# Second layer's input projection: units in the order queries, keys, latents, values, with norm, turn and eviction work spread between them

## What is computed

```
h = rms_norm(x, n1_g) * (1.0 + sc1) + sh1
z = h @ w_in                                   # 1024 -> 1952 columns
dq, dk, dv, qa, kva, kr = jnp.split(z, ODD_SPLITS, axis=-1)   # 512, 512, 512, 256, 128, 32
dq = rms_norm(dq.reshape(B, S, DIFF_HEADS, 2, DIFF_HD), dq_g)
dk = rms_norm(dk.reshape(B, S, DIFF_HEADS, 2, DIFF_HD), dk_g)
ckv = rms_norm(kva, kva_g)
q = rms_norm((rms_norm(qa, qa_g) @ w_qb).reshape(B, S, MLA_HEADS, MLA_QK), mq_g)
...
dq = apply_rope(dq, cos, sin)                  # latent tokens only
dk = apply_rope(dk, cos, sin)
lam = jnp.exp(jnp.sum(lq1 * lk1)) - jnp.exp(jnp.sum(lq2 * lk2)) + LAMBDA_INIT
o1 = attend(dq[:, :, :, 0:1], k_d[:, :, :, 0], v_d)
o2 = attend(dq[:, :, :, 1:2], k_d[:, :, :, 1], v_d)
```

## Time and profile before

| | us |
|---|---|
| median of 3 runs (lowest, highest) | 1410.58 (1409.72, 1410.68) |
| profiled execution | 1410.37 |
| its span in the trace | 1408.5 |
| TensorE busy | 1280.5 (91%) |
| VectorE busy | 896.6 (64%) |
| ScalarE busy | 758.0 (54%) |
| TensorE on the chain that ended last | 75% |

### The profile page before, as it was taken

How to read it: one execution, slowest core, us unless ns; L and a number is a source line. 1 busy time by engine, 2 the same in 40 slices (tenths; PEclk the granted TensorE clock), 3 DMA queues, 4 the chain that set the end, 5 groups by cost and what they waited for, 6 DMA issues and landing times.

```text
span 1408.5 us, 19755 instructions
## 1 busy us (share of the span) xinstructions
PE 1280.5 (91%) x7731; PEld 1125.5 (80%) x7731; DVE 896.6 (64%) x1149; ACT 758.0 (54%) x1098; POOL 293.4 (21%) x248
## 2 busy tenths in 40 slices
PE   5896899899999998987968898999999999999895
PEld 3794567799899987984656697889989989889793
DVE  1448756453433345665575524889789789799776
ACT  3467664542323225323355324677777877777673
POOL 0368850100110012000023021011312303213113
PEclk9997899999999998995986796999999999999998
DMA  9842993153443354421921121699899899899882
GB/s 311 238 134 88 303 331 122 59 165 98 143 147 106 98 170 136 125 70 62 333 64 61 31 83 47 224 332 336 263 347 322 277 337 327 277 340 319 285 294 79
DMA packets 178361, 277.67 MB, mean 197 GB/s; under 512 B 7121, under 2 KB 105193, under 8 KB 178265
## 3 DMA queue, kind: packets, MB, share of 16 engines
q1 hardware_dynamic: 176040, 269.87, 57.8%
q0 software_dynamic: 2224, 6.49, 1.7%
HBM read 274.02 MB, written 2.31 MB: 196 GB/s over the span
## 4 chain that ended last, share of the span: by engine, by line
PE 75%; DVE 10%; issue 8%; ACT 4%; DMA 2%; POOL 1%; SPq 1%; DVEq 0%; ACTq 0%; POOLq 0%
PE psB L1994 5%; PE psB L1996 5%; PE psB L1995 5%; PE psB L1497 4%; PE psB L1499 4%; PE psB L1498 4%; PE psA L1994 4%; PE psA L1996 4%; PE psA L1995 4%; PE psB L1583 3%; PE psB L1638 2%; PE psB L1733 2%; PE psB L1732 2%; PE psB L1734 2%; PE psA L1618 2%
## 5 line engine op out<-in xcount | busy, mean ns | idle before, releaser
L2619 DVE TENSOR_TENSOR Wl<-raw,Wh 128x1408 fp32r<-128x1408 f32 (+2 forms) x144 | 247.1, 1739 | 57.5 <-ACT Wh L1397 56.7
L2057 DVE TENSOR_TENSOR Wl<-raw,Wh 128x2048 fp32r<-128x2048 f32 (+4 forms) x64 | 133.9, 2097 | 141.6 <-ACT Wh L1039 141.2
L1397 ACT CAST Wh<-raw 128x1408 fp32r<-128x1408 f32 (+2 forms) x144 | 197.0, 1375 | 27.5 <-PE psA L1996 14.5
L1039 ACT CAST Wh<-raw 128x2048 fp32r<-128x2048 f32 (+4 forms) x64 | 109.9, 1724 | 116.4 <-PE psB L1734 64.2
L1994 PE MATMUL psA<-Wh,hTh 128*128 128x352 f32 x360 | 118.3, 329 | 0.7 <-ACT hTl L1403 0.7
L1996 PE MATMUL psA<-Wh,hTl 128*128 128x352 f32 x360 | 116.7, 324 | 0.0
L1995 PE MATMUL psA<-Wl,hTh 128*128 128x352 f32 x360 | 116.1, 323 | 0.0
L935 POOL TENSOR_TENSOR yc<-yc,work 128x414 f32<-128x414 f32 x90 | 101.1, 1145 | 52.8 <-ACT work L1138 50.2
L1497 PE MATMUL psB<-Wh,hTh 128*128 128x256 f32 (+2 forms) x356 | 104.2, 293 | 7.8 <-DVE Wl L2057 2.0
L1498 PE MATMUL psB<-Wl,hTh 128*128 128x256 f32 (+2 forms) x356 | 103.6, 291 | 0.0
L1499 PE MATMUL psB<-Wh,hTl 128*128 128x256 f32 (+2 forms) x356 | 103.6, 291 | 0.0
(11 more groups left out here) (376 smaller groups left out, 3398.7 us busy)
## 6 DMA issues: line engine op xcount, KB each, us to landing
raw<-in_l_moe_w SPq DMA_DIRECT2D x108, 704.0 KB, 5.7
raw<-in_l_ada_w SPq DMA_DIRECT2D x48, 1024.0 KB, 6.0
raw<-in_l_ffn_w SPq DMA_DIRECT2D x28, 1024.0 KB, 5.3
raw<-in_l_moe_w SPq DMA_DIRECT2D x27, 768.0 KB, 6.4
gate_b<-in_l_moe_w SPq DMA_DIRECT2D x18, 768.0 KB, 7.0
gate_b<-in_l_moe_w SPq DMA_DIRECT2D x18, 704.0 KB, 5.8
raw_tail<-in_l_moe_w SPq DMA_DIRECT2D x18, 704.0 KB, 5.6
raw<-in_l_w_in SPq DMA_DIRECT2D x11, 1024.0 KB, 5.6
```

The lines of the kernel that those rows point to most:

```text
L1039: act.copy(hi_of(u), raw_of(u)).then_inc(hi_ready, 1)
L1397: act.copy(half_of(Wh, h), raw_half(h)).then_inc(half_hi, 1)
L2057: dve.tensor_tensor(lo_of(u), raw_of(u), hi_of(u).bitcast(F32), ALU.subtract).then_inc(lo_ready, 1)
L2619: dve.tensor_tensor(half_of(Wl, h), raw_half(h), half_of(Wh, h).bitcast(F32), ALU.subtract).then_inc(half_lo, 1)
```

## The change

The eight units now come in the order queries, queries, keys, keys, latents, latents, values, values. VectorE empties the banks of units 0 and 1 only, ScalarE those of units 2 to 7 (18 banks), each time behind the items of that unit. All six items lie between units: 0 and 1 at unit 2, item 2 at unit 3, items 3 and 4 at unit 4, item 5 at unit 5. The latent norms lie at unit 6. TensorE makes the seven groups of `TURNS1` between units: two behind unit 3, one behind 4, three behind 5, one behind 6. Only the latents' three groups are left behind unit 7. `lam`'s sums move to VectorE's list at step 17 of `attend(0)`, its Exp to ScalarE's list there, two steps later. The writes of the new keys, values and latents to memory stay where they were in GpSimd's list.

```diff
-                unit(KD, 256, (0, w_in[:, :, 1536:1792]))
-                unit(KD, 256, (0, w_in[:, :, 1696:1952]))
-                for j in range(6):
-                    unit(KD, 256, (0, w_in[:, :, j * 256:(j + 1) * 256]))
+                for at in (0, 256, 512, 768, 1536, 1696, 1024, 1280):
+                    unit(KD, 256, (0, w_in[:, :, at:at + 256]))
...
-        Z_LAT, Z1, Z2 = NT + 1, NT + 1, 3 * NT + 1
+        Z_LAT, Z1, Z2 = 3 * NT + 1, NT, 3 * NT + 1
...
-        ITEM_AT = {4: 0, 5: 1, 6: 2, 7: 3}
+        ITEMS1 = {2: (0, 1), 3: (2,), 4: (3, 4), 5: (5,)}
+        LATENT_AT, ACT_UNITS = 6, 2
         TURNS1 = [(0, 0), (0, 1), (0, 2), (1, 0), (1, NT), (1, 1), (1, 2)]
+        TURNS1_AFTER = {3: (0, 1), 4: (2,), 5: (3, 4, 5), 6: (6,)}
...
+                    if a == 0 and s == LAMBDA_AT + 2:
+                        act.wait_ge(lam_in, 1)
+                        act.activation(stats[:, 90:92], stats[:, 88:90], ACT.Exp).then_inc(lam_e, 1)
...
-            table_of(ACT.Exp)
-            act.wait_ge(lam_in, 1)
-            act.activation(stats[:, 90:92], stats[:, 88:90], ACT.Exp).then_inc(lam_e, 1)
+            g0 = first["prep1"]["T"]
             for j in range(8):
                 if j < 7:
                     step(base["in", 1] + j)
-                if j in (1, 2):
-                    qk_root((QR, KVR)[j - 1], NT)
-                if j in ITEM_AT:
-                    act.wait_ge(psB_free, first["in1"]["B"] + NT * j)
-                    squares(1, ITEM_AT[j])
+                for n in TURNS1_AFTER.get(j - 1, ()):
+                    k, t = TURNS1[n]
+                    transposed_in(g0 + n, (qT1, kT1)[k][:, :, t * P:(t + 1) * P])
+                act.wait_ge(psB_free, first["in1"]["B"] + NT * j)
+                for m in ITEMS1.get(j, ()):
+                    squares(1, m)
+                for m in ITEMS1.get(j, ()):
                     qk_root(HD, 8)
-            g0 = first["prep1"]["T"]
-            act.wait_ge(psB_free, first["in1"]["B"] + 24)
-            squares(1, 4)
+                if j == LATENT_AT:
+                    qk_root(QR, NT)
+                    qk_root(KVR, NT)
+                if j >= ACT_UNITS:
+                    for t in range(NT):
+                        act.wait_ge(psB_full, first["in1"]["B"] + NT * j + t + 1)
+                        act.copy(in1_columns(j, t), in1_bank(j, t)).then_inc(psB_free, 1)
...
             for j in range(1, 8):
                 unit_b(base["in", 1] + j, first["in1"]["B"] + NT * j, (hTh, hTl))
-            pe.wait_ge(cache_in, 96)
+                for n in TURNS1_AFTER.get(j, ()):
+                    turn1(n)
...
-                dve.wait_ge(psB_free, first["in1"]["B"] + NT * j)
-                if j in (1, 2):
-                    at, n, name = ((0, QR, "l1_mla_q_a_norm_g"), (QR, KVR, "l1_mla_kv_a_norm_g"))[j - 1]
...
+                dve.wait_ge(psB_free, first["in1"]["B"] + NT * (j if j == LATENT_AT else min(j, 4)))
+                if j == LATENT_AT:
+                    for at, n, name in ((0, QR, "l1_mla_q_a_norm_g"), (QR, KVR, "l1_mla_kv_a_norm_g")):
...
-                if j in ITEM_AT:
-                    item1(ITEM_AT[j])
-                for t in range(NT):
...
+                for m in ITEMS1.get(j, ()):
+                    item1(m)
+                for t in range(NT) if j < ACT_UNITS else ():
+                    dve.wait_ge(psB_full, first["in1"]["B"] + NT * j + t + 1)
+                    dve.tensor_copy(in1_columns(j, t), in1_bank(j, t)).then_inc(psB_free, 1)
```

More of the change, by code:

```diff
@@ L59 @@
 OUT_SPLIT = 23
+LAMBDA_AT = 17
 AHEAD = S - 1
@@ L724, in lat_columns, with in1_columns, in1_bank @@
             return kv[:, t, j * 512:(j + 1) * 512]
-        ITEM_AT = {4: 0, 5: 1, 6: 2, 7: 3}
+        ITEMS1 = {2: (0, 1), 3: (2,), 4: (3, 4), 5: (5,)}
+        LATENT_AT, ACT_UNITS = 6, 2
         TURNS1 = [(0, 0), (0, 1), (0, 2), (1, 0), (1, NT), (1, 1), (1, 2)]
+        TURNS1_AFTER = {3: (0, 1), 4: (2,), 5: (3, 4, 5), 6: (6,)}
+        def in1_columns(j, t):
+            if j in (4, 5):
+                return zm[:, t, 0:256] if j == 4 else zm[:, t, 256:416]
+            at = j * 256 if j < 4 else (j - 2) * 256
+            return zd[:, t, at:at + 256]
+        def in1_bank(j, t):
+            n = units[base["in", 1] + j][2]
+            return psB[(first["in1"]["B"] + NT * j + t) % 3][:, n - 160 if j == 5 else 0:n]
         blocks = ([(0, d // 2 + YC * (d % 2)) for d in range(FRONT)] + [(0, u) for u in range(FRONT, ADA)] +
@@ L1855, in _, with turn1 @@
             norm(1, 0, rows_products(base["in", 1], first["in1"]["B"]))
+            def turn1(n):
+                k, t = TURNS1[n]
+                g = first["prep1"]["T"] + n
+                if t < NT:
+                    pe.wait_ge(z_ready, Z1 + NT * k + t + 1)
+                else:
+                    pe.wait_ge(cache_in, 96)
+                free_t(g)
+                for j in range(4):
+                    if t == NT:
+                        src = cdk[:, j * P:(j + 1) * P]
+                    else:
+                        src = zd[:, t, k * DIFF_W + j * P:k * DIFF_W + (j + 1) * P]
+                    last = pe.transpose(psT[g % 2][:, j * P:(j + 1) * P], src, ident)
+                last.then_inc(psT_full, 1)
             for j in range(1, 8):
                 unit_b(base["in", 1] + j, first["in1"]["B"] + NT * j, (hTh, hTl))
-            pe.wait_ge(cache_in, 96)
+                for n in TURNS1_AFTER.get(j, ()):
+                    turn1(n)
             g0 = first["latT"]["T"]
@@ L1867, in _ @@
                 last.then_inc(psT_full, 1)
-            g0 = first["prep1"]["T"]
-            pe.wait_ge(psT_free, g0)
-            for n, (k, t) in enumerate(TURNS1):
-                if t < NT:
-                    pe.wait_ge(z_ready, Z1 + NT * k + t + 1)
-                free_t(g0 + n)
-                for j in range(4):
-                    if t == NT:
-                        src = cdk[:, j * P:(j + 1) * P]
-                    else:
-                        src = zd[:, t, k * DIFF_W + j * P:k * DIFF_W + (j + 1) * P]
-                    last = pe.transpose(psT[(g0 + n) % 2][:, j * P:(j + 1) * P], src, ident)
-                last.then_inc(psT_full, 1)
-            pe.wait_ge(psT_free, g0 + 7)
+            pe.wait_ge(psT_free, first["prep1"]["T"] + 7)
+            pe.wait_ge(psB_free, first["in1"]["B"] + 24)
             attend(1)
@@ L2254, in attend, with lambda_sums @@
                     o_low(a, NT - 1)
+            def lambda_sums():
+                for n, (q, k) in enumerate((("l1_lambda_q1", "l1_lambda_k1"), ("l1_lambda_q2", "l1_lambda_k2"))):
+                    link(dve.tensor_tensor(scr[:, 0:HD], G[q], G[k], ALU.mult))
+                    ins = dve.tensor_reduce(stats[:, 88 + n:89 + n], scr[:, 0:HD], AX.X, ALU.add)
+                    if n == 0:
+                        link(ins)
+                ins.then_inc(lam_in, 1)
             def o_low(a, t):
@@ L2446, in _ @@
             ffn()
-            for n, (q, k) in enumerate((("l1_lambda_q1", "l1_lambda_k1"), ("l1_lambda_q2", "l1_lambda_k2"))):
-                link(dve.tensor_tensor(scr[:, 0:HD], G[q], G[k], ALU.mult))
-                ins = dve.tensor_reduce(stats[:, 88 + n:89 + n], scr[:, 0:HD], AX.X, ALU.add)
-                if n == 0:
-                    link(ins)
-            ins.then_inc(lam_in, 1)
             dve.wait_ge(x_added, 18)
```

27 lines of the change are left out of this document (8 added, 19 removed).

## The result

| | before | changed |
|---|---|---|
| first comparison, median (lowest, highest), 5 executions each | 1410.35 (1409.59, 1410.68) | 1389.55 (1388.72, 1396.96) |
| their ratio, with 95% interval | | 0.9867 (0.985 to 0.9884) |
| profiled execution | 1410.37 | 1396.96 |
| its span | 1408.5 | 1395.1 |
| its mean granted clock | 0.932 | 0.933 |

A forecast was written before the change was run, and what follows sets the result against it. TensorE was taken as the bound, losing time idle or at half clock in layer 1's first part. 13.9 us to the first Exp, plus 0.5 for clock, less 0.1, made 14.3: 1396.1 profiled, 1396.3 median, range 1391 to 1401.

The forecast's parts named there:

- lambda sums out of the norm: Norm ahead of layer 1's units: without the sums on VectorE, scaled tokens are ready 1.0 us sooner (0.3 to 1.1).
- lambda sums into `attend(0)`: VectorE at step 17 of `attend(0)`: 2.1 us of sums nearly covered by idle time, cost 0 to 0.6 us, taken 0.1.
- bank waits of units 2 and 6: TensorE's idle 1.63 and 1.27 us at these units' starts, from banks VectorE emptied late, would go: gain 2.9 us.
- seven groups of turns between units: Turns on TensorE moved between units at full clock, about 0.6 us each: 4.3 us added before unit 7's end.
- end of unit 7 to first Exp: Tail behind unit 7, the main term: first Exp 4.5 us behind the unit instead of 18.8, gain 14.3 us.
- clock in the attention: `attend(1)`: clock falls again and returns with the asides; steps still at full clock gain a little, taken 0.5 us.
- Theory C: From a rerun's expectation, not the prediction: layer 0's attention with the lambda sums is sometimes disturbed, 1.2 us of the difference.
- The walk along the banks: Bank-freeing times counted from unit 1's end: unit 3's first bank 0 to 0.3 us tight, VectorE later one to ten us ahead.
- Rivals 2 and 5: Late ScalarE bank copies hold TensorE, 1398.5 to 1403.5 us, chance 0.16; latents not ready behind unit 7, near 1410, 0.02.
- Rival 4: Bank waits bring the clock down inside units; 4 us waits at units 3, 4 and 5 give 1415.8 us; chance 0.03.
- Rival 3: ScalarE's table load behind unit 7: the skill page's drain puts the first Exp 1.4 us later, 1397.7 us; chance 0.04.
- The first rival: Clock stays full into layer 1's first attention: 3 to 6 us more gain, 1390.5 to 1393.5 us; chance 0.15.

## Why the prediction came out as it did, step by step

The sum held: 14.3 forecast, 13.4 to 14.7 in the stage by the traces, 15 by all executions. Its terms, one by one:

| step | forecast | measured |
|---|---|---|
| lambda sums out of the norm | +1.0 (0.3 to 1.1) | +0.2 |
| lambda sums into `attend(0)` | -0.1 | 0.0 |
| bank waits of units 2 and 6 | +2.9 | +2.9 |
| new bank waits | 0 to 0.3, none in the sum | 0 |
| seven groups of turns between units | -4.3 | -3.3 |
| end of unit 7 to first Exp | +14.3 (18.8 to 4.5) | +14.46 (18.84 to 4.38) |
| clock in the attention | +0.5 | 0.0 to +0.3 (table load to first aside, three traces) |

**Lambda out of the norm, mis-sized.** The step took VectorE's own list as the limit, with ScalarE's root as the next thing behind it. Its bracket named the right limit as its lower end ("if GpSimd's last add is held up by VectorE's earlier work"), and that is what came out. VectorE's timeline of the changed kernel:

```profile
543.92 0.69 DVE L2358 TENSOR_TENSOR work<-psB,gate_b 128x512 f32<-128x512 f32 x1 [0.81 <-PE psB L1749]
546.36 0.16 DVE L2133 RECIPROCAL stats<-stats 128x1 f32<-128x1 f32 x1 [1.75 <-POOL x L962]
...
548.53 0.75 DVE L2134 TENSOR_SCALAR work<-x,stats 128x1024 f32<-128x1024 f32 x1
```

The add ends 1.7 us behind the last gate in both kernels, and the sums ended 0.3 us behind the add. Only these 0.3 could go. A row of GpSimd, one line of the same stretch, would have told it.

**Lambda into `attend(0)`.** The sums took 0.21 to 0.23 us each where they had taken up to 0.93, the minima came at 190.82, and the probabilities' first transpose at 193.21. Both lie 1.65 us behind their places in the earlier trace rows, and so does all of this stage ahead of the sums. From these minima to the last gate of the feed-forward it is 353.6 us before and 353.1 in the changed kernel: the sums cost nothing, and the 1.2 us of Theory C lie ahead of them.

**The walk along the banks.** It put the last root ahead of unit 2's copies at 8.2 and the first bank's freeing at 8.5 to 8.6, against 8.65 wanted. ScalarE's timeline:

```profile
581.76 0.30 ACT L1071 ACTIVATE stats<-stats,cst 128x8 f32<-128x8 f32 x1 [2.57 <-DVE stats L2153]
581.97 0.99 ACT L1356 COPY zd<-psB 128x256 f32<-128x256 f32 x3
```

Unit 3 starts without a wait. The margin that the prediction called the tightest held, and the later ones grew as it said: VectorE ends the latents' norms at 619.12, 10 us ahead of their transposes. Rivals 2 and 5 are out. Rival 4's mechanism is not: with VectorE on the copies, the waits of 4.2 and 2.9 us did bring the clock down inside the units. The prediction wanted them 4 us long at three units to end slower than before; 4.2 and 2.9 us at two units left 3.5 to 4 us of the gain. It took 5 us of work at half clock for each return, and the trace has 4.6 and 3.4.

**The turns, mis-sized.** TensorE's timeline at the two denser places:

```profile
591.17 1.04 PE L1885 MATMUL psT<-cst,zd 128*128 128x128 f32 x8
591.96 0.36 PE L1512 MATMUL psB<-Wh,hTh 128*128 128x256 f32 x1
```

```profile
609.75 0.60 PE L1885 MATMUL psT<-cst,zd 128*128 128x128 f32 x4
610.18 0.60 PE L1885 MATMUL psT<-cst,cdk 128*128 128x128 f32 x4
611.12 0.63 PE L1885 MATMUL psT<-cst,zd 128*128 128x128 f32 x4 [0.33 <-ACT kT L1281]
611.50 0.36 PE L1512 MATMUL psB<-Wh,hTh 128*128 128x256 f32 x1
```

Read by starts, two groups take 0.79 us and the three 1.75, in which lies the wait for a bank of `psT` (0.33 by the row, 0.5 by the starts); the two single ones take 0.36 each. That is 3.3 us for seven groups, 0.36 to 0.43 each without the wait. The forecast's 0.6 came from a length in the earlier trace rows. A length runs on into the next instruction's; the distance between starts is what the engine pays.

**The tail.** Right in size and in its parts: the cast 2.4 us behind the unit, the table load beneath which scores and minima are done, Exp at once behind it. The load takes 1.28 us, and the next instruction on ScalarE starts 1.29 us after the load's start. The Trainium skill (ScalarE: Activation LUTs, section "What ACT_TABLE_LOAD costs") adds a drain of about 1.38 us to a switch; by that the first Exp would have stood an estimated 5.8 us behind the unit. The trace doesn't agree: it has 4.38. Rival 3 is out.

**The clock.** The first rival is false: the clock fell in all three traces of the changed kernel, 5 to 6 us behind unit 7, and came back 2 to 3.5 us behind the first aside, as it had before (2.9 us). Forced to stay up, it brought nothing net. Its price of 3 to 6 us was never tested free of the products that hold it up, so what full clock alone would be worth there stays open.

**The level, the step that failed.** The prediction took three executions within 1 us as the spread of the kernel and converted the sum into a time to within 2 us. The term for the clock's luck was missing: by the fit above it was worth 6 us in the first comparison. The range of 10 us was made of costs alone, and the first median fell 1.5 us below it. One pair of traces gave this gain to 1 or 2 us; the three series of five or six executions put it at 19.0, 14.3 and 12.3.

**The two halves need each other.** ScalarE on the banks alone is worth 1 to 3 us, which its interval doesn't tell from nothing; order, items and turns without it about 4; both 13 to 15. With the items between units, VectorE must be relieved of the copies, or TensorE waits for the items there instead of in the tail. With the items still in the tail, relieving VectorE shortens nothing that is waited for.

## What to carry to other kernels

Work that one engine must finish ahead of a serial stage (norms and turns ahead of an attention) belongs under the matmuls of the units that don't need it, which asks for the units in the order of need; the bank copies must then go to an engine that has room beside that chain, or the wait only moves. Here that was ScalarE, which has the squares and roots of the items but idles 1.5 to 4.4 us ahead of each root. Before an operation is counted as a gain because it leaves an engine's list, look for every engine that the next instruction waits for, not only its own. Where executions of one program differ by more than the effect, compare traces between fixed points, take more than one trace of each kernel, and repeat both on one chip.

## What the runs showed of the hardware

- One program's time at half clock varies from execution to execution: 159 to 206 us for the kernel before, with times from 1399 to 1416 us.
- A wait of TensorE of 4.2 us inside dense work brought 7 us at 0.50, beginning 2.0 us into it. One of 2.9 us brought 3 us, beginning 1.4 us behind its end. The waits of 1.27 and 1.63 us in the kernel before brought none.
- In the norm, behind the same wait of 5.5 to 5.7 us, the clock came back some 5.6 us behind the tokens in three of the traces compared here and 8.1 and 8.5 us in the two others, with the same list of instructions but for the lambda sums. From the tokens to the end of unit 7 that is 79.2 against 80.2 us in the changed kernel and 78.1 against 80.1 in the kernel before.
- Useless products held the clock at 1.00 from 556 to 805 us, and the kernel was 9 us slower than with such products in `attend(1)` alone. There, with the products in front of it, the second pair of scores started 7.8 us behind unit 7 instead of 5.3.
- Sums over 128x64 took VectorE 0.66 and 0.93 us for the product ahead of the norm, with GpSimd adding into `x` at the same time, and 0.21 and 0.23 us in `attend(0)`.
